# Two of three projection steps moved behind the level's second pair of products in a gated delta rule head

## The chip, the cores and the metric

The kernel runs on one core of one Trainium2 chip (trn2). The metric is the device time of one execution in microseconds, the median of three runs. Differences within 0.2% are about what repeated runs of one kernel show.

## The reference, cut to what matters

The whole program is two transformer blocks in fp32: a gated delta rule block with memory attention and a feed-forward part, then a convolution block and a sparse attention block. The change touches only the gated delta rule (8 heads of 128, 512 tokens). For each head the reference projects the input, runs a short convolution and SiLU over the rows, and solves a unit lower triangular system before it scans over the tokens:

```python
qkv = jax.nn.silu(causal_dwconv(qkv, conv_w))
q, k, v = jnp.split(qkv, [GDN_KW, 2 * GDN_KW], axis=-1)
...
lower = jnp.where(strict, bc[..., :, None] * kk * decay, 0.0)
sol = lax.linalg.triangular_solve(lower + jnp.eye(CHUNK), rhs, left_side=True, lower=True, unit_diagonal=True)
...
v_new = u_n - w_n @ state
o_n = qg_n @ state + p_n @ v_new
state = state * gl_n + kg_n.T @ v_new
```

## The kernel before, in words

The program is written engine by engine, with semaphores between the engines and every engine's order written out by hand. Heads 1 to 6 run as a hardware loop; head 0 and head 7 are peeled (`gdn_tensor`, `gdn_scalar`, `gdn_vector`).

**What one head does.** The triangular matrix is inverted by doubling, in four blocks of 128 tokens side by side in one 128x512 tile. `LEVELS` is 7, so `head_tensor` runs six levels (`lv` 0 to 5). One level is:

1. TensorE forms A from the level's mask of the lower matrix and U, four 128x128 products into bank 4 (line 722).
2. ScalarE copies bank 4 to the tile `As` (line 852).
3. TensorE forms T and As for U into bank 5 (line 730, called U's products here) and, in levels 0 to 4, As and T for T into bank 6 (line 735, T's products).
4. VectorE subtracts bank 5 from `U` (line 931) and bank 6 from `T` (line 934), forms the next mask (line 937), and in between does work for other heads. A of the next level waits for the subtraction of U.

**The projection steps.** While head `h` is inverted, TensorE also computes the projections of head `h+1`: four output tiles (key, value, query, gate z), each of eight steps. One step is three 128x512 products, high by high, high by low and low by high part of the split fp32 numbers (lines 281 to 283). `gap(n)` runs the next `n` of the 32 steps, so the calls of `gap` say where they lie between the head's own products. Nine steps lie ahead of level 0. The second tile ends with step 16, which is the first step of level 2, and the third tile ends with step 24, which is the last step of level 4. Head 7 projects the memory queries in their place.

**What hangs on a finished tile.** ScalarE takes it out of its bank (`take_row`, line 770). VectorE then convolves it over four taps (`conv_steps`): line 799 is the first tap, line 801 the other three, each after a wait for the one before. All of it reads and writes SBUF alone. ScalarE applies SiLU (line 782). GpSimd (POOL) waits for the end of the tile and then splits the weights of the tile after next, a cast (line 226) and a subtraction (line 246), both in SBUF. For the third tile the calls on VectorE stand in the loop over levels:

```python
dve.wait_ge(s_["U_done"], h * 6 + (lv + 1))
V.tensor_tensor(U, U, bank[5], ALU.subtract)   # 931, U_moved
...                                            # 934, 937
conv(lv // 2, 2)                               # two taps of tile lv // 2
```

So the first two taps of the third tile come after T's subtraction in level 4, ahead of U's subtraction in level 5. The last two taps come behind it, then one 128x512 product of the next head's gate rows (line 877), and then the first block of the scan.

**The scan.** Four blocks of 128 tokens follow one another. TensorE forms the new values (line 749, which in block 0 waits for the last subtraction of U), does one step, and waits for VectorE's copy `v_new` (line 952) before line 759 adds to the state. In the scan lie steps 28 to 32.

Of the kernel before, what the change touches and what calls it, by code (L numbers as in the profile page):

```python
# [44 lines left out]
LEVELS = 7  # L45
# [84 lines left out]
def program(nc, t, out):  # L130

    with ExitStack() as ctx:
# [515 lines left out]
        def group_chunks(pe, g):  # L648

            for j in range(GROUP_TILES):  # L650
                unit = g * GROUP_TILES + (seg_g.unit0 + j)
                pe.wait_ge(tile_taken, g * GROUP_TILES + (seg_g.tile0 + j - 1))
                for k in range(DT):
                    products(pe, seg_g, unit, (seg_g.unit0 + j) % 2, 0, bank[(seg_g.tile0 + j) % 2][:, :],
                             lambda k: X_R[:, k], lambda k: X_L[:, k], True, True, ks=(k, k + 1))
                    yield

        def key_norm_tensor(pe, g):
            pe.wait_ge(s_["keys_squared"], g * 2 + 1)
            nc.tensor.matmul(bank[5][:, :], ones, g_["sq_k"][:, :], start=True, stop=True).then_inc(s_["norm_summed"], 1)  # L660

        def query_norm_tensor(pe, g):
            pe.wait_ge(s_["keys_squared"], g * 2 + 2)
            nc.tensor.matmul(bank[6][:, :], ones, g_["sq_q"][:, :], start=True, stop=True).then_inc(s_["norm_summed"], 1)

        def output_norm_tensor(pe, n):

            pe.wait_ge(s_["o_squared"], n)
            nc.tensor.matmul(bank[2][:, :], ones, o_squares, start=True, stop=True).then_inc(s_["o_summed"], 1)

        def head_tensor(pe, h, g, first, last):
            chunks = group_chunks(pe, g)

            def gap(n):
                for _ in range(n):
                    next(chunks, None)

            pe.wait_ge(s_["gate_rows_ready"], h + 1)
            nc.tensor.matmul(bank[4][:, :], ones, g_["D_E"][:, :], start=True, stop=True).then_inc(s_["rows_done"], 1)
            pe.wait_ge(s_["norms_rooted"], h * 2 + 2)  # L680
            pe.wait_ge(s_["silu_done"], h * 3 + 2)
            for b in range(NB):
                mm = nc.tensor.transpose(bank[5][:, b * P:(b + 1) * P], acts[1][:, b * P:(b + 1) * P], ident)
            mm.then_inc(s_["v_turned"], 1)
            gap(1)
            pe.wait_ge(s_["keys_ready"], h + 1)
            for b in range(NB):
                kb = g_["keys"][:, b * P:(b + 1) * P]
                mm = nc.tensor.matmul(bank[7][:, b * P:(b + 1) * P], kb, kb, start=True, stop=True)
            mm.then_inc(s_["kk_done"], 1)  # L690
            for b in range(NB):
                mm = nc.tensor.transpose(bank[6][:, b * P:(b + 1) * P], g_["keys"][:, b * P:(b + 1) * P], ident)
            mm.then_inc(s_["k_turned"], 1)
            gap(4)
            if not first:
                output_norm_tensor(pe, h)
            gap(2)
            pe.wait_ge(s_["T_ready"], h + 1)
            for b in range(NB):
                mm = nc.tensor.transpose(bank[3][:, b * P:(b + 1) * P], g_["T"][:, b * P:(b + 1) * P], ident)  # L700
            mm.then_inc(s_["T_turned"], 1)
            gap(2)
            pe.wait_ge(s_["row_decay_ready"], h + 1)
            pe.wait_ge(s_["v_beta_ready"], h + 1)
            pe.wait_ge(s_["k_gained_ready"], h + 1)
            pe.wait_ge(s_["queries_ready"], h + 1)
            if not first:
                pe.wait_ge(s_["o_rooted"], h)
            for b in range(NB):
                here = slice(b * P, (b + 1) * P)  # L710
                mm = nc.tensor.matmul(bank[2][:, here], g_["keys"][:, here], g_["queries"][:, here], start=True, stop=True)
            mm.then_inc(s_["qk_done"], 1)
            for lv in range(LEVELS - 1):
                joins = g_["low_a"] if lv % 2 == 0 else g_["low_b"]
                pe.wait_ge(s_["low_ready"], h * 6 + (lv + 1))
                if lv == 0:
                    pe.wait_ge(s_["U_ready"], h + 1)
                else:
                    pe.wait_ge(s_["U_moved"], h * 6 + lv)
                for b in range(NB):  # L720
                    here = slice(b * P, (b + 1) * P)
                    mm = nc.tensor.matmul(bank[4][:, here], joins[:, here], g_["U"][:, here], start=True, stop=True)  # L722
                mm.then_inc(s_["A_done"], 1)
                gap(3 if lv < LEVELS - 2 else 1)
                pe.wait_ge(s_["A_ready"], h * 6 + (lv + 1))
                if lv:
                    pe.wait_ge(s_["T_moved"], h * 5 + lv)
                for b in range(NB):
                    here = slice(b * P, (b + 1) * P)
                    mm = nc.tensor.matmul(bank[5][:, here], g_["T"][:, here], g_["As"][:, here], start=True, stop=True)  # L730
                mm.then_inc(s_["U_done"], 1)
                if lv < LEVELS - 2:
                    for b in range(NB):
                        here = slice(b * P, (b + 1) * P)
                        mm = nc.tensor.matmul(bank[6][:, here], g_["As"][:, here], g_["T"][:, here], start=True, stop=True)  # L735
                    mm.then_inc(s_["T_done"], 1)
            gap(2)
            pe.wait_ge(s_["pT_ready"], h + 1)
            pe.wait_ge(s_["q_decayed_ready"], h + 1)
            pe.wait_ge(s_["U_moved"], h * 6 + 6)  # L740
            for b in range(NB):
                here = slice(b * P, (b + 1) * P)
                if b:
                    pe.wait_ge(s_["S_ready"], h * 3 + b)
                    nc.tensor.matmul(bank[7][:, 0:P], g_["keys"][:, here], g_["S"][:, :], start=True, stop=True).then_inc(s_["kS_done"], 1)
                    gap(1)
                    pe.wait_ge(s_["X_ready"], h * 3 + b)
                rhs = g_["X"][:, :] if b else g_["v_beta"][:, here]
                nc.tensor.matmul(bank[2][:, 0:P], g_["U"][:, here], rhs, start=True, stop=True).then_inc(s_["v_done"], 1)
                if b:  # L750
                    nc.tensor.matmul(bank[3][:, here], g_["S"][:, :], g_["q_decayed"][:, here], start=True, stop=False)
                if not last and b == 1:
                    key_norm_tensor(pe, g)
                elif not last and b == 2:
                    query_norm_tensor(pe, g)
                gap(1)
                pe.wait_ge(s_["v_ready"], h * 4 + (b + 1))
                if b < NB - 1:
                    nc.tensor.matmul(bank[4][:, 0:P], g_["k_gained"][:, here], g_["v_new"][:, :], start=True, stop=True).then_inc(s_["S_sum_done"], 1)
                mm = nc.tensor.matmul(bank[3][:, here], g_["v_new"][:, :], g_["pT"][:, here], start=b == 0, stop=True)  # L760
                if b == NB - 1:
                    mm.then_inc(s_["o_done"], 1)
            gap(40)
# [198 lines left out]
        def gdn_tensor(pe):  # L962
            for _ in group_chunks(pe, 0):
                pass
            gates_tensor(pe)
            key_norm_tensor(pe, 0)
            query_norm_tensor(pe, 0)
            head_tensor(pe, 0, 1, True, False)
            with pe.Fori(1, HEADS - 1) as h:
                head_tensor(pe, h, h + 1, False, False)  # L970
            head_tensor(pe, HEADS - 1, HEADS, False, True)
            output_norm_tensor(pe, HEADS)
# [1233 lines left out]
```

## Time and profile before

| what | value |
|---|---|
| median of 3 runs | 2411.93 us (2408.79 to 2413.52) |
| the profiled execution: time, span | 2413.52 us, 2411.6 us |
| PE busy | 2254.8 us, 93% of the span |
| VectorE, ScalarE, POOL busy | 50%, 40%, 32% |
| mean granted clock of TensorE | 0.972 of full speed |
| stretch of the eight heads, from the trace | 124 to 558 us of the span, some 54 us a head |

The engines are named PE (TensorE matmul), PEld (its weight load), DVE (VectorE), ACT (ScalarE), POOL (GpSimd). In a row of the windows each engine's busy time is followed by its count of instructions, in the order PE, PEld, DVE, ACT, POOL, then the granted clock, the share of the DMA engines and GB/s. A row of the timeline has the start in the span, the duration, the engine, the line, the operation, the tiles and how often it is merged; in brackets stands the idle time before it and what ended it. The ends of matmuls are modelled, so the distance between two starts is the better measure of how long PE took.

### The profile page before, as it was taken

What the parts mean: (1) busy time and instruction counts of PE and PEld (TensorE: products, weight loads), DVE (VectorE), ACT (ScalarE), POOL (GpSimd) and SP (SyncE); (2) the same over time, 40 slices, a digit from 0 to 9 for tenths busy, and PEclk for the clock granted to TensorE, in tenths of its full rate; (3) what the DMA queues carried; (4) which work ended last, traced back from release to release, by engine and by line L of the source; (5) the groups of instructions that cost most, each with busy time, mean ns of one, the idle gap of its engine ahead of it and who ended that gap; (6) DMA issues with size and microseconds to landing.
All of it is one profiled execution on the core that took longest, in us unless ns stands there. A gap on an engine that the chain in (4) does not pass through costs nothing.

```text
span 2411.6 us, 31521 instructions
## 1 busy us (share of the span) xinstructions
PE 2254.8 (93%) x10534; PEld 1788.9 (74%) x10534; DVE 1195.1 (50%) x1906; ACT 971.1 (40%) x1612; POOL 768.7 (32%) x336
## 2 busy tenths in 40 slices
PE   3899999998899999989979999999999989999997
PEld 2677777776678888858847888888766657888886
DVE  6366666654243332269964333325566665333322
ACT  4434444433342222265544444222455454444322
POOL 2522222221334444400014444444310103444442
PEclk7999999998999999999989999999999999999999
DMA  3211111111222233211102222322100002322322
GB/s 121 101 36 36 43 35 43 35 38 61 94 70 96 96 99 107 89 44 53 52 19 87 100 96 99 118 99 73 62 18 9 17 10 75 100 96 96 104 99 76
DMA packets 43626, 168.83 MB, mean 70 GB/s; under 512 B 4848, under 2 KB 4912, under 8 KB 43056
## 3 DMA queue, kind: packets, MB, share of 16 engines
q1 hardware_dynamic: 43056, 163.82, 20.3%
q10 hardware_dynamic: 512, 4.24, 0.5%
q8 instruction: 35, 0.57, 0.1%
q14 instruction: 23, 0.19, 0.0%
HBM read 165.95 MB, written 2.10 MB: 70 GB/s over the span
## 4 chain that ended last, share of the span: by engine, by line
PE 80%; DVE 8%; issue 5%; ACT 4%; POOL 1%; DMA 0%; DVEq 0%; ACTq 0%; POOLq 0%; SPq 0%
PE bank L281 21%; PE bank L283 21%; PE bank L282 21%; PE bank L1796 2%; PE bank L722 2%; PE bank L730 2%; PE bank L735 1%; POOL WL L246 1%; ACT Pr L1846 1%; PE bank L1760 1%; PE bank L1778 1%; PE bank L1313 1%; PE bank L1315 1%; PE bank L1314 1%; DVE Pr L1917 1%
## 5 line engine op out<-in xcount | busy, mean ns | idle before, releaser
L246 POOL TENSOR_TENSOR WL<-raw,WR 128x1024 fp32r<-128x1024 f32 (+2 forms) x274 | 706.9, 2580 | 1022.8 <-ACT WR L242 1018.1
L281 PE MATMUL bank<-XR,WR 128*128 128x512 f32 x1528 | 627.6, 411 | 30.1 <-DVE XL L426 15.3
L283 PE MATMUL bank<-XR,WL 128*128 128x512 f32 x1528 | 600.0, 393 | 0.0
L282 PE MATMUL bank<-XL,WR 128*128 128x512 f32 x1528 | 599.0, 392 | 0.0
L242 ACT ACTIVATE WR<-raw 128x1024 fp32r<-128x1024 f32 (+2 forms) x230 | 256.2, 1114 | 754.7 <-PE bank L283 747.1
L281 PEld LDWEIGHTS bank<-XR,WR 128*128 128x128 f32 x1528 | 289.9, 190 | 103.8 <-issue 31.9
L281 PE MATMUL bank<-MR,WR 128*128 128x512 f32 (+1 forms) x856 | 337.4, 394 | 16.1 <-DVE ML L1482 7.5
L282 PEld LDWEIGHTS bank<-XL,WR 128*128 128x128 f32 x1528 | 290.2, 190 | 64.4 <-issue 9.9
L283 PEld LDWEIGHTS bank<-XR,WL 128*128 128x128 f32 x1528 | 289.1, 189 | 62.0
L282 PE MATMUL bank<-ML,WR 128*128 128x512 f32 (+1 forms) x856 | 333.4, 390 | 0.0
L283 PE MATMUL bank<-MR,WL 128*128 128x512 f32 (+1 forms) x856 | 333.2, 389 | 0.0
L226 POOL CAST WR<-raw 128x1024 fp32r<-128x1024 f32 (+1 forms) x58 | 61.7, 1064 | 594.4 <-PE bank L283 509.7
L281 PEld LDWEIGHTS bank<-MR,WR 128*128 128x128 f32 x856 | 163.5, 191 | 52.7 <-issue 13.2
L1269 DVE TENSOR_TENSOR f_up<-bank,R 128x512 f32<-128x512 f32 x66 | 45.6, 691 | 302.7 <-PE bank L283 302.7
L283 PEld LDWEIGHTS bank<-MR,WL 128*128 128x128 f32 x856 | 163.9, 191 | 32.7
L282 PEld LDWEIGHTS bank<-ML,WR 128*128 128x128 f32 x856 | 164.1, 192 | 30.9 <-issue 0.2
L402 DVE TENSOR_TENSOR ACC<-ACC,SQ 128x512 f32<-128x512 f32 (+1 forms) x56 | 86.5, 1545 | 144.0 <-ACT SQ L391 142.7
L1274 DVE TENSOR_TENSOR ML<-f_mid,MR 128x512 f32 x66 | 123.1, 1865 | 64.5 <-ACT MR L1252 64.5
L1212 DVE TENSOR_TENSOR hT<-bank,hT 128x512 f32 (+1 forms) x24 | 16.6, 692 | 161.0 <-PE bank L283 161.0
L1846 ACT ACTIVATE Pr<-Pr,stats 128x512 f32<-128x512 f32 (+3 forms) x128 | 70.3, 550 | 58.2 <-DVE stats L1917 58.2
L1267 DVE TENSOR_TENSOR f_gate<-bank,R 128x512 f32<-128x512 f32 x66 | 45.6, 691 | 92.1 <-PE bank L283 72.0
L426 DVE SCALAR_TENSOR_TENSOR XL<-hT,params,XR (+1 forms) x40 | 69.3, 1733 | 33.8 <-ACT XR L422 33.8
(295 smaller groups left out, 2774.6 us busy)
## 6 DMA issues: line engine op xcount, KB each, us to landing
raw<-w SPq DMA_DIRECT2D x224, 512.0 KB, 3.3
raw<-w SPq DMA_DIRECT2D x48, 704.0 KB, 4.0
raw<-w SPq DMA_DIRECT2D x16, 384.0 KB, 3.0
hT<-xT SPq DMA_DIRECT2D x1, 2048.0 KB, 8.0
hT<-xT ACTq DMA_DIRECT2D x1, 2048.0 KB, 7.9
out<-Y SPq DMA_DIRECT2D x8, 256.0 KB, 2.0
memT<-memT ACTq DMA_DIRECT2D x1, 1024.0 KB, 8.0
phi<-phi ACTq DMA_DIRECT2D x1, 1024.0 KB, 6.1
```

What stands on the lines that cost most here:

```text
L226: nc.gpsimd.tensor_copy(WR[:, here], raw[:, here]).then_inc(high_split, 1)
L242: nc.scalar.activation(WR[:, here], raw[:, here], ACT.Identity).then_inc(high_ahead, 1)
L246: nc.gpsimd.tensor_tensor(WL[:, here], raw[:, here], WR[:, here].bitcast(F32), ALU.subtract).then_inc(weight_split, 1)
L281: nc.tensor.matmul(into, wr, xr(k0 + k), start=start, stop=False)
L282: nc.tensor.matmul(into, wr, xl(k0 + k), start=False, stop=False)
L283: mm = nc.tensor.matmul(into, wl, xr(k0 + k), start=False, stop=stop)
L402: nc.vector.tensor_tensor(ACC[:, 0:width], ACC[:, 0:width], SQ[:, parity * SEQ:parity * SEQ + width], ALU.add).then_inc(summed, 1)
L426: nc.vector.scalar_tensor_tensor(dst, src, gain, high.bitcast(F32), ALU.mult, ALU.subtract).then_inc(input_ready, 1)
L722: mm = nc.tensor.matmul(bank[4][:, here], joins[:, here], g_["U"][:, here], start=True, stop=True)
L730: mm = nc.tensor.matmul(bank[5][:, here], g_["T"][:, here], g_["As"][:, here], start=True, stop=True)
L1274: nc.vector.tensor_tensor(cols(ML, n), f_mid[:, :], cols(MR, n).bitcast(F32), ALU.subtract).then_inc(mid_low, 1)
L1846: ins = nc.scalar.activation(here, here, ACT.Exp, bias=stat(idx, 0)[:, b:b + 1], scale=-1.0, accum_out=stat(idx, 1)[:, b:b + 1])
```

## The change

In `head_tensor` each of levels 0 to 4 had three steps between A and U's products. Now one step lies there, and two lie behind T's products, ahead of the next level's A. Level 5 had one step behind A and two behind the loop; the two now stand inside the loop, at the same place. The order within the 32 steps and their number stay as they are, and no other engine's program is changed.

```diff
@@ -721,7 +721,7 @@
                     here = slice(b * P, (b + 1) * P)
                     mm = nc.tensor.matmul(bank[4][:, here], joins[:, here], g_["U"][:, here], start=True, stop=True)
                 mm.then_inc(s_["A_done"], 1)
-                gap(3 if lv < LEVELS - 2 else 1)
+                gap(1)
                 pe.wait_ge(s_["A_ready"], h * 6 + (lv + 1))
                 if lv:
                     pe.wait_ge(s_["T_moved"], h * 5 + lv)
@@ -734,7 +734,7 @@
                         here = slice(b * P, (b + 1) * P)
                         mm = nc.tensor.matmul(bank[6][:, here], g_["As"][:, here], g_["T"][:, here], start=True, stop=True)
                     mm.then_inc(s_["T_done"], 1)
-            gap(2)
+                gap(2)
             pe.wait_ge(s_["pT_ready"], h + 1)
             pe.wait_ge(s_["q_decayed_ready"], h + 1)
             pe.wait_ge(s_["U_moved"], h * 6 + 6)
```

## Rows read from the trace of the kernel before

**Rows 1.** The page: the chain that ended last, shares of the span by engine.

```profile
PE 80%; DVE 8%; issue 5%; ACT 4%; POOL 1%; DMA 0%; DVEq 0%; ACTq 0%; POOLq 0%; SPq 0%
```

**Rows 2.** Timeline of PE, level 1 of one head and the A of level 2.

```profile
297.80 1.13 PE L722 MATMUL bank<-U,low_b 128*128 128x128 f32 x8
298.69 0.47 PE L281 MATMUL bank<-XR,WR 128*128 128x512 f32 x1
...
300.85 1.05 PE L730 MATMUL bank<-As,T 128*128 128x128 f32 x8
301.74 1.06 PE L735 MATMUL bank<-T,As 128*128 128x128 f32 x8
302.80 1.13 PE L722 MATMUL bank<-U,low_a 128*128 128x128 f32 x8
```

**Rows 3.** Timeline of PE, same head: level 4, level 5, start of the scan.

```profile
312.76 1.13 PE L722 MATMUL bank<-U,low_a 128*128 128x128 f32 x8
...
315.57 0.39 PE L283 MATMUL bank<-XR,WL 128*128 128x512 f32 x1
...
317.72 1.13 PE L722 MATMUL bank<-U,low_b 128*128 128x128 f32 x8
...
319.61 1.15 PE L730 MATMUL bank<-As,T 128*128 128x128 f32 x8
320.52 0.47 PE L281 MATMUL bank<-XR,WR 128*128 128x512 f32 x1
...
321.99 0.38 PE L749 MATMUL bank<-v_beta,U 128*128 128x128 f32 x2
...
324.03 0.49 PE L759 MATMUL bank<-v_new,k_gained 128*128 128x128 f32 x2 [0.96 <-DVE v_new L952]
```

**Rows 4.** Timeline of VectorE in the same head.

```profile
304.04 2.35 DVE L801 SCALAR_TENSOR_TENSOR act<-pre,params,act 128x512 f32<-128x512 f32 x2
...
318.39 1.52 DVE L799 TENSOR_SCALAR act<-pre,params 128x512 f32<-128x512 f32 x1
320.05 0.75 DVE L801 SCALAR_TENSOR_TENSOR act<-pre,params,act 128x512 f32<-128x512 f32 x1
320.93 0.69 DVE L931 TENSOR_TENSOR U<-U,bank 128x512 f32<-128x512 f32 x1
...
323.69 0.28 DVE L952 COPY v_new<-bank 128x128 f32<-128x128 f32 x1
```

**Rows 5.** Timeline of ScalarE in the same head, levels 4 and 5.

```profile
316.00 0.60 ACT L770 ACTIVATE pre<-bank 128x512 f32<-128x512 f32 x1 [1.47 <-PE bank L283]
316.49 0.62 ACT L782 ACTIVATE act<-act 128x512 f32<-128x512 f32 x1
318.89 0.60 ACT L852 ACTIVATE As<-bank 128x512 f32<-128x512 f32 x1 [1.77 <-PE bank L722]
```

**Rows 6.** Timeline of POOL: two splits of this head, one in each of the next two.

```profile
304.81 1.04 POOL L226 CAST WR<-raw 128x1024 fp32r<-128x1024 f32 x1 [9.64 <-PE bank L283]
305.92 2.69 POOL L246 TENSOR_TENSOR WL<-raw,WR 128x1024 fp32r<-128x1024 f32 x1
...
316.13 1.04 POOL L226 CAST WR<-raw 128x1024 fp32r<-128x1024 f32 x1 [7.51 <-PE bank L283]
317.25 2.38 POOL L246 TENSOR_TENSOR WL<-raw,WR 128x1024 fp32r<-128x1024 f32 x1
...
360.30 1.04 POOL L226 CAST WR<-raw 128x1024 fp32r<-128x1024 f32 x1 [9.64 <-PE bank L283]
...
414.11 1.04 POOL L226 CAST WR<-raw 128x1024 fp32r<-128x1024 f32 x1 [9.65 <-PE bank L283]
```

**Rows 7.** Windows at that head's end, and at a later one's: busy by engine, PEclk.

```profile
332.70:336.10 3.40, 2.29 (x11) 1.41 (x10) 1.76 (x4) 3.09 (x5) 3.29 (x2) 1.00 0.00 0
336.10:339.50 3.40, 3.40 (x11) 2.35 (x10) 2.53 (x5) 1.29 (x4) 0.00 (x0) 0.50 0.45 154
445.30:448.70 3.40, 3.40 (x10) 2.18 (x9) 2.43 (x4) 1.19 (x3) 0.04 (x1) 0.51 0.47 154
```

## The prediction

> **What bounds the kernel now.** I read the page first: the chain that ended last is 80% PE and 8% VectorE [rows 1], so what PE does costs its full time, and a change of its order can only win where PE waits. Then I read PE's timeline through one head, level by level, because the diff moves steps there. In level 1, A starts at 297.80, the three steps at 298.69, U's products at 300.85, T's at 301.74, and the next A at 302.80 [rows 2]. The four parts take 0.89, 2.16, 0.89 and 1.06 us, together 5.00. T's products alone would need what U's need, 0.89, so PE stands 0.17 us ahead of the next A, and the wait that the code has there is the one for U's subtraction. A level is otherwise all work: the change has 0.17 us a level to win, five times a head.
>
> Then the tail of the head. Behind the levels PE waits 0.96 us for the copy `v_new` [rows 3], and the VectorE rows say why that is late: the first tap took 1.52 us where the next, with more to read, took 0.75; it ended 0.28 us after POOL's subtraction (317.25 + 2.38 = 319.63), so I take it that it waited for it, then one tap, U's subtraction, two more taps, a 0.7 us product, and the copy, end to end from 318.39 to 323.97 [rows 4, 6]. From 318.4 on, VectorE and not PE sets the time of this head. Six of the other heads (0 to 6 without this one) show the same pattern; head 7 has no taps.
>
> I call A's start of level 4, 312.76, zero of the tail. There the last of the three steps' products starts at 2.81, A of level 5 at 4.96, U's products at 6.85, line 749 at 9.23 and line 759 at 11.27 [rows 3].
>
> **Term 1, the levels.** Removed: 0.17 us ahead of each next A. With two steps there, A comes at the earliest 1.47 us after T's products, and U's subtraction ends long before.
> Added: a wait for `As` ahead of U's products. Level 5 already has one step there and shows the price: A at 317.72, copy 318.89 to 319.49, U's products at 319.61, that is A + 1.89 [rows 3, 5]. A group of two steps takes 321.99 - 320.52 = 1.47, one of three 2.16, so a step takes 0.69 and a group 0.08 on top; one step would let U's products start at 0.89 + 0.77 = 1.66. PE waits 0.23 us. Three steps (2.16) hid the copy wholly. Splitting them into 0.77 + 1.47 = 2.24 costs another 0.08.
> The new level: 1.89 + 0.91 + 0.89 + 1.47 = 5.16 us, where 0.91 is U's products in level 5 (319.61 to 320.52). Before, levels 1 to 4 took (317.72 - 297.80)/4 = 4.98. So +0.18 us a level: the win of 0.17 is paid back by 0.23 + 0.08 and the 0.02 of U's products, with 0.02 for the other levels' shorter wait. For levels 0 to 3 of eight heads that is 32 x 0.18 = 5.8, and head 7's level 4 adds 0.2: **+6 us**. Here two waits are exchanged, and the step count on PE is the same.
>
> **Term 2, what the moved third tile does to the tail (levels 4 and 5 of heads 0 to 6).** The third tile ends with the last step of level 4, which is moved behind U's and T's products. Its last product starts at 5.16 - 0.23 = 4.93 (0.23 is the distance of such products) instead of 2.81, so everything that hangs on the tile is 2.12 us later. In order:
> - ScalarE's take follows by 316.00 - 315.57 = 0.43: 5.36 to 5.96. Its SiLU is issued 0.49 later, and `As` of level 5 can follow at about 6.37. It wants to start at 5.16 + 1.17 = 6.33, so these two ahead of it in ScalarE's queue cost nearly nothing [rows 5]. U's products start at about 7.1.
> - POOL's cast follows by 316.13 - 315.57 = 0.56: 5.49 to 6.53; its subtraction wants to start at 6.60 [rows 6].
> - VectorE's first tap, queued behind T's subtraction, now waits for the take and starts near 6.1, while the cast runs. Level 2 of before shows this meeting: the second tap of the pair from 304.04 should have ended at about 305.7, but ended at 306.39, 0.54 after the cast (305.85), and the subtraction on POOL, issued at 305.92, took 2.69 instead of 2.38, ending 2.22 after the tap [rows 4, 6]. So the two do not share: each waits for the other's whole instruction. The first tap ends at 6.53 + 0.29 = 6.82, and POOL's subtraction about 2.22 later, 9.04. (In before the first tap was the only one that met POOL in the tail.)
> - The second tap, which needs the first one's result, asks at 6.95 and finds POOL inside. It ends 0.55 after it: 9.59. Before, it ended at 320.80, or 8.04 [rows 4].
> - Queued behind it on VectorE: U's subtraction of level 5, the last two taps, the product of line 877, `v_new`. From the end of this tap to line 759 before were 324.03 - 320.80 = 3.23 us. So line 759 starts at 12.82 instead of 11.27: **+1.55 us a head**, seven heads, **+11 us**. PE waits there in two places: for U ahead of line 749 (free at 9.53, U ready at about 10.55) and for `v_new` (about 11.5 to 12.8), 2.3 us together instead of 0.96.
> The subtractions read PSUM and show 0.69 beside POOL too, so I charge them nothing. In the GPSIMD Engine Reference of the Trainium skill, section "Key points", VectorE contends with GpSimd in its two-port modes or with two SBUF inputs; by that rule U's subtraction, with one PSUM input, is indeed free while the taps are not.
> The bounds of this term: nothing, if the tap meets no POOL instruction (VectorE would then reach `v_new` at about the old 11.3), and 2.1 us a head, if the first tap misses the slot between cast and subtraction: it then ends 0.29 after POOL at 8.98, and line 759 is at 8.98 + 0.29 + 0.14 + 0.75 + 3.23 = 13.4. I take 1.55, because level 2's rows show the slot given to VectorE when it asks during the cast.
> The level 2 tile (step 16) is the first of its group before and after, so its take and split keep their place; its taps move off POOL, and POOL falls instead on the mask of line 937, which nobody waits for until level 4.
>
> **Term 3, PE's clock.** In this head the clock fell from full (2.4 GHz) to half (1.2 GHz) at 336.1, just behind a stretch in which PE was busy 2.29 of 3.40 us [rows 7], its gaps 1.11 us together. The head-to-head distance was then 360.30 - 304.81 = 55.49 us, against 414.11 - 360.30 = 53.81 without it [rows 6]: 1.68 us for one half-clock stretch. One more head's end has such a stretch, at 445.3 [rows 7]; I found none at the other heads' ends. After the change, term 2's waits of 1.0 and 1.3 us lie close together with one step between, which is more idle time in one place than ahead of 336.1. I expect one stretch at half clock at nearly every scan's start in heads 0 to 6. Part of it falls on the wait itself and costs nothing, so I take 1.3 us each, from bounds of 0 and 1.68: **+9 us**.
> In TensorE: Matmul & The Clock Gate of the Trainium skill, the section on HAM oscillation asks only that long gaps be avoided, longer than any here; by that rule this term would be zero and the time about 2429. The row at 336.1 already differs from it, since the clock fell there behind gaps of 1.11 us in all. The next section of that page, on a second failure mode, has the clock swing from frequent short idle times too, and by that one the term stands.
>
> The sum: 5.9 + 10.9 + 9.1 = 25.9 us. The profiled execution has a span of 2411.6 and a time of 2413.52; with the sum that is 2439.4. It is the slowest of the three, 1.6 over the median, and the sum on the median is 2437.8. I say **2438 us**.
>
> **The rivals.**
> - *No more half-clock stretches.* For it: most heads of before kept full clock through the same scan. Against: the new gaps are twice as long. Terms 1 and 2 alone: 2411.9 + 16.8 = 2429 us.
> - *The tail hides it.* Only term 1 stays. The tap and POOL would have to miss each other, which 6.1 against 5.49 to 6.53 speaks against. 2411.9 + 5.9 = 2418 us.
> - *The first tap loses the slot.* Term 2 becomes 7 x 2.1 = 15, and the clock term stays: 2442 us. The first tap must start after 6.6, half a microsecond later than I have it; the semaphore and two register steps ahead of it could take part of that.
> - *Within 0.2%.* The copy of `As` is less late than in level 5, and the tail is hidden: the levels then cost 0 to 0.1 us each, 2412 to 2416.
> - *Faster.* One step hides the copy of `As` after all. The place is the wait ahead of U's products; it is decided where a step of 0.77 us outlasts the 1.0 us from A's end to U's start (319.61 - 318.61). If it did, a level would win 0.17 and pay 0.08: 40 x -0.09 = -3.6 us; with the two half-clock stretches of before gone as well (-3.4), 2411.9 - 7.0 = 2405. Level 5's row speaks against it.
>
> **How the numbers follow.** My forecast 0.45; no extra half clock 0.22; only the levels 0.14; the slot lost 0.08; within 0.2% 0.06; faster 0.05. About 0.2%, 4.8 us, is what this kernel's runs can tell from no change, so "only the levels" at 2418 lies just outside it, and I move 0.02 of it inside: faster 0.05, same 0.08, slower 0.87. The range reaches from the levels alone, 2417, to the slot lost with the full 1.68 us for each half-clock stretch, 2412 + 6 + 15 + 12 = 2445, and one or two more stretches at the heads' ends: 2417 to 2447.
>
> **What the changed profile would show.** Term 1: A to A 5.16 us in levels 0 to 3; an idle time of 0.2 us ahead of line 730 put down to `As`; none ahead of line 722. Term 2: line 799 starting during POOL's cast of the third tile and the line 801 behind it stretched to 2.6 us; idle time ahead of line 749 put down to U's subtraction in seven heads; 12.8 us from level 4's A to line 759. Term 3: half clock beginning within some 5 us behind that wait, seven times. I am wrong if level 4's A to line 759 stays near 11.3, if the taps are not stretched, or if U's products start less than 1.8 us behind A.

## The result, and the profile after

The changed kernel takes 2428.42 us (2422.97 to 2431.35), the kernel before 2411.93. The ratio is 1.0069, 95% interval 1.0052 to 1.0087: slower by 16.5 us. The profiled execution has a span of 2424.5 us and a time of 2426.29, 12.9 us of span over the one of before. So the direction was forecast, and the size lies at the rival "no more half-clock stretches" (2429), not at the 2438 of the forecast. In the table of the experiments one run of the kernel before (4144 us) and two of `taps_late` (6911 and 10599 us) stand far above all others and are left out of the ratios, though not of the medians.

PE's timeline, level 2 of the same head (head 3), to be held against [rows 2]. The columns are the same.

```profile
308.89 1.05 PE L722 MATMUL bank<-U,low_a 128*128 128x128 f32 x8
309.69 0.48 PE L281 MATMUL bank<-XR,WR 128*128 128x512 f32 x1
...
310.70 1.15 PE L730 MATMUL bank<-As,T 128*128 128x128 f32 x8
311.69 1.06 PE L735 MATMUL bank<-T,As 128*128 128x128 f32 x8
312.51 0.48 PE L281 MATMUL bank<-XR,WR 128*128 128x512 f32 x1
...
313.98 1.05 PE L722 MATMUL bank<-U,low_b 128*128 128x128 f32 x8
```

A to A is 5.09 us. One step lies between 309.69 and 310.46, and U's products start 1.81 behind A, 0.24 later than the step allows. The two steps behind T's products end where the next A starts, so nothing is waited for there.

VectorE and POOL in the same level:

```profile
308.90 1.64 DVE L801 SCALAR_TENSOR_TENSOR act<-pre,params,act 128x512 f32<-128x512 f32 x2
311.89 0.69 DVE L931 TENSOR_TENSOR U<-U,bank 128x512 f32<-128x512 f32 x1 [1.36 <-PE bank L730]
...
313.39 1.48 DVE L937 TENSOR_TENSOR low_a<-lower,table 128x512 f32<-128x512 f32 x1
```

POOL's subtraction lies from 311.93 to 314.32 there. U's subtraction takes its 0.69 us beside it, and the mask of line 937 ends 0.55 us behind it.

The tail, same head, PE, to be held against [rows 3].

```profile
319.07 1.05 PE L722 MATMUL bank<-U,low_a 128*128 128x128 f32 x8
...
324.17 1.05 PE L722 MATMUL bank<-U,low_b 128*128 128x128 f32 x8
...
326.10 1.15 PE L730 MATMUL bank<-As,T 128*128 128x128 f32 x8 [0.18 <-ACT As L852]
...
329.55 0.46 PE L749 MATMUL bank<-v_beta,U 128*128 128x128 f32 x2 [0.90 <-DVE U L931]
...
331.82 0.69 PE L759 MATMUL bank<-v_new,k_gained 128*128 128x128 f32 x2 [1.11 <-DVE v_new L952]
```

VectorE, the same stretch, to be held against [rows 4].

```profile
325.11 0.71 DVE L799 TENSOR_SCALAR act<-pre,params 128x512 f32<-128x512 f32 x1 [1.45 <-ACT pre L770]
325.96 2.63 DVE L801 SCALAR_TENSOR_TENSOR act<-pre,params,act 128x512 f32<-128x512 f32 x1
328.72 0.69 DVE L931 TENSOR_TENSOR U<-U,bank 128x512 f32<-128x512 f32 x1
...
331.48 0.28 DVE L952 COPY v_new<-bank 128x128 f32<-128x128 f32 x1
```

ScalarE, the take of the third tile, its SiLU and the copy of level 5, against [rows 5].

```profile
324.37 0.60 ACT L770 ACTIVATE pre<-bank 128x512 f32<-128x512 f32 x1 [3.60 <-PE bank L283]
324.86 0.62 ACT L782 ACTIVATE act<-act 128x512 f32<-128x512 f32 x1
325.38 0.59 ACT L852 ACTIVATE As<-bank 128x512 f32<-128x512 f32 x1
```

POOL: the split in level 2 of heads 1 to 3, and the one behind head 3's third tile, against [rows 6].

```profile
197.96 1.04 POOL L226 CAST WR<-raw 128x1024 fp32r<-128x1024 f32 x1 [9.80 <-PE bank L283]
...
254.97 1.04 POOL L226 CAST WR<-raw 128x1024 fp32r<-128x1024 f32 x1 [9.80 <-PE bank L283]
...
310.81 1.04 POOL L226 CAST WR<-raw 128x1024 fp32r<-128x1024 f32 x1 [9.80 <-PE bank L283]
...
324.50 1.04 POOL L226 CAST WR<-raw 128x1024 fp32r<-128x1024 f32 x1 [10.18 <-PE bank L283]
325.62 2.43 POOL L246 TENSOR_TENSOR WL<-raw,WR 128x1024 fp32r<-128x1024 f32 x1
```

Read the four groups from PE's tail to POOL together. The take starts at 324.37, the first tap follows it at 325.11 in the midst of POOL's cast (324.50 to 325.54) and ends 0.28 us behind the cast. The second tap then stands from 325.96 to 328.59, 0.54 us behind the end of POOL's subtraction at 328.05. U's subtraction, which PE waits for, is queued behind that tap. From A of level 4 to line 759 it is 331.82 - 319.07 = 12.75 us, against 11.27 [rows 3]. The waits ahead of line 749 sum to 6.4 us over 7 heads, those ahead of line 759 to 7.7 us over 7 (6.6 before); the first did not exist before.

Windows of PE's clock at this head's scan start, against [rows 7].

```profile
329.00:332.40 3.40, 1.74 (x8) 1.29 (x9) 2.62 (x5) 1.35 (x3) 0.00 (x0) 0.94 0.43 154
332.40:335.80 3.40, 3.40 (x13) 2.77 (x13) 0.94 (x3) 1.19 (x1) 0.00 (x0) 0.56 0.00 0
```

PE had 1.74 us of work in the first window. Its mean granted clock of 0.94 puts the fall to half (1.2 GHz) into its last 0.4 us, at about 332. Such a fall at the scan's start happened in heads 1, 3 and 5 (at about 219, 332 and 445). The casts give the price: head 1 to head 2 is 254.97 - 197.96 = 57.01 us, head 2 to head 3 55.84, so 1.17 us a stretch. The two stretches of before at heads' ends (1.6 to 1.7 each) are gone.

From head 0's first A to head 7's it is 392.8 us (524.15 - 131.40), against 379.3 before (511.37 - 132.07): 13.4 us more. What follows head 7's first A takes 1900.3 us in both traces. In the repeat of the changed kernel the two times are 392.7 and 1903.7 us. So the traces put 13 to 14 us down to the change, and the rest of the 16.5 is not found in the part of the program that was changed.

### The profile page after: what moved, and what is told of

It is laid out like the page before. It is cut to its first block, busy times and chain, and to the rows that moved or that the text cites. A ratio compares the mean times of both kernels' runs of the same rounds, so it can differ in the third digit from the quotient of the medians.

```text
span 2424.5 us, 31521 instructions
## 1 busy us (share of the span) xinstructions
PE 2257.6 (93%) x10534; PEld 1782.7 (74%) x10534; DVE 1204.0 (50%) x1906; ACT 970.3 (40%) x1612; POOL 767.1 (32%) x336
## 4 chain that ended last, share of the span: by engine, by line
PE 79%; DVE 9%; issue 5%; ACT 4%; POOL 1%; DMA 1%; DVEq 0%; ACTq 0%; POOLq 0%; SPq 0%
PE bank L281 21%; PE bank L283 21%; PE bank L282 21%; PE bank L1796 2%; PE bank L730 2%; PE bank L722 2%; PE bank L735 1%; DVE act L801 1%; POOL WL L246 1%; ACT Pr L1846 1%; PE bank L1760 1%; PE bank L1778 1%; PE bank L1313 1%; PE bank L1315 1%; PE bank L1314 1%
```

## The experiments

Each ratio is to the kernel before, run on the same chip (its median there 2411.2 to 2411.6). "A to A" (the mean) and "tail" (A of level 4 to line 759) are of heads 1 to 6 of the trace. "Heads" is the time from head 0's first A to head 7's in the trace, with the count of half-clock stretches inside it. What follows head 7's first A differs by up to 8 us between the traces (1897.6 to 1905.9 us), so this column tells the kernels apart better than the medians do.

| kernel | median us | ratio, 95% interval | A to A, levels 1 to 3 | tail | heads (half-clock stretches) |
|---|---|---|---|---|---|
| before | 2411.93 | | 4.98 | 11.27 | 379.3 (2) |
| changed | 2428.42 | 1.0069, 1.0052 to 1.0087 | 5.09 | 12.75 | 392.8 (3) |
| changed, again | 2427.04 | 1.0066, 1.0048 to 1.0084 | 5.09 | 12.75 | 392.7 (3) |
| levels_0_3 | 2413.42 | 1.0003, 0.9991 to 1.0014 | 5.09 | 11.20 | 379.9 (1) |
| level_4 | 2424.96 | 1.0048, 1.0032 to 1.0064 | 4.97 | 12.83 | 390.1 (2) |
| after_short | 2413.43 | 1.0008, 0.9995 to 1.0020 | 5.09 | 11.31 | 379.3 (0) |
| before_short | 2412.66 | 0.9997, 0.9982 to 1.0011 | 4.98 | 11.16 | 378.8 (2) |
| after_filler | 2424.05 | 1.0053, 1.0034 to 1.0072 | 5.09 | 12.75 | 389.2 (0) |
| after_taps_late | 2413.65 | 1.0019, 1.0006 to 1.0032 | 5.09 | 11.47 | 379.7 (0) |
| two_one | 2408.41 | 0.9987, 0.9971 to 1.0003 | 4.76 | 11.20 | 369.9 (0) |
| taps_late | 2403.01 | 0.9964, 0.9948 to 0.9979 | 4.98 | 10.14 | 369.2 (1) |
| taps_late_2_1 | 2392.00 | 0.9929, 0.9909 to 0.9948 | 4.76 | 10.09 | 361.4 (0) |

**Which levels cost: levels_0_3.** Against the kernel before:

```diff
-                gap(3 if lv < LEVELS - 2 else 1)
+                gap((1, 1, 1, 1, 3, 1)[lv])
...
-            gap(2)
+                gap((2, 2, 2, 2, 0, 2)[lv])
```

> One step ahead of U's products and two behind in levels 0 to 3 alone; level 4 keeps its three steps ahead. Theory (two terms: a wait for As in each level, and a third tile that ends late): only the first term is left, 5.09 against 4.97 us from A to A in levels 1 to 4, so about +4 us, 2416; from A of level 4 to line 759 stays 11.27 us; the tap of line 801 after the first is not stretched; no half clock at a scan's start. Rival (the split of the levels alone costs, wherever it stands): four fifths of the change's 16.5 us, +13 us, with the tail of the head longer too.

PE's timeline, head 3:

```profile
315.98 1.05 PE L722 MATMUL bank<-U,low_a 128*128 128x128 f32 x8
...
327.18 0.49 PE L759 MATMUL bank<-v_new,k_gained 128*128 128x128 f32 x2 [0.94 <-DVE v_new L952]
```

The tail stays short (11.20 us) and the first tap is again the only one in it that meets POOL. The split levels are longer, 5.09 us, and level 4 with its three steps is 0.08 shorter than before (4.88), so a head without half clock takes 54.25 us against 53.9. Over seven heads that is some 2.4 us. It does not show in the time of this trace's heads (379.9 us against 379.3) because one half-clock stretch at a head's end, at 283.1, stands there in place of two. The median moved by less than can be told. The rival is out: the split of the levels costs a little, and it is not where most of the 16.5 us lie.

**Level 4 alone: level_4.** The same two lines with `(3, 3, 3, 3, 1, 1)` and `(0, 0, 0, 0, 2, 2)`.

> The split in level 4 alone. Theory: the tail is whole, 12.75 instead of 11.27 us from A of level 4 to line 759 in seven heads, +10.5 us, and some heads have half clock at the scan's start (0 to 4, 1.2 us each) in place of the two at heads' ends before: +8 to +14 us, 2420 to 2426. Rival (the levels cost, the tail little): +3 us.

```profile
319.86 1.13 PE L722 MATMUL bank<-U,low_a 128*128 128x128 f32 x8
...
332.69 0.49 PE L759 MATMUL bank<-v_new,k_gained 128*128 128x128 f32 x2 [1.12 <-DVE v_new L952]
```

One level out of five brings 13.4 of the 16.5 us in the medians and 10.8 of the 13.4 in the traces' heads, and the tail is 12.83 us. The trace has no half clock at a scan's start, although the waits are the same as in the changed kernel (0.90 us ahead of line 749 and 1.12 ahead of line 759). It has two stretches at heads' ends, as before; this is the window of the first:

```profile
232.50:235.90 3.40, 3.40 (x12) 2.38 (x11) 2.41 (x5) 1.15 (x4) 0.00 (x0) 0.53 0.51 154
```

**Is it POOL, or the late take: after_short.** The changed kernel with POOL's subtraction cut short in this stage. It leaves out 7/8 of the low parts of the projection weights, which stay stale.

```diff
-            low_unit(seg, slot)
+            low_unit(seg, slot, P if seg is SEG["gdn"] else None)
...
-        def low_unit(seg, slot):
-            here = slice(slot * SLOT, slot * SLOT + seg.kt * P)
+        def low_unit(seg, slot, cut=None):
+            here = slice(slot * SLOT, slot * SLOT + (cut or seg.kt * P))
```

> The changed kernel, with POOL's subtraction (line 246) for the weights of the gated delta rule's projections done on 128 of 1024 columns, so that the rest of the low parts is stale; the cast stays whole. Theory (the taps wait for POOL's whole instruction): the second tap takes 0.75 instead of 2.63 us, PE's waits ahead of lines 749 and 759 shrink, 11.2 to 11.4 us from A of level 4 to line 759 instead of 12.75, and the time is 10 us under the changed kernel's, about 2417. Rival (it is the late take of the tile and not POOL): 12.5 us or more stays, and the time is within 3 us of the changed kernel's 2428.

PE, VectorE and POOL of head 3, one timeline each:

```profile
314.20 1.05 PE L722 MATMUL bank<-U,low_a 128*128 128x128 f32 x8
...
325.50 0.49 PE L759 MATMUL bank<-v_new,k_gained 128*128 128x128 f32 x2 [0.85 <-DVE v_new L952]
```

```profile
320.21 0.71 DVE L799 TENSOR_SCALAR act<-pre,params 128x512 f32<-128x512 f32 x1 [1.43 <-ACT pre L770]
321.07 0.75 DVE L801 SCALAR_TENSOR_TENSOR act<-pre,params,act 128x512 f32<-128x512 f32 x1
322.39 0.69 DVE L931 TENSOR_TENSOR U<-U,bank 128x512 f32<-128x512 f32 x1 [0.57 <-PE bank L730]
```

```profile
320.73 0.51 POOL L246 TENSOR_TENSOR WL<-raw,WR 128x128 fp32r<-128x128 f32 x1
```

The first tap still meets the cast (0.71 us), the second runs free in 0.75, U's subtraction now waits for PE rather than PE for it, and the tail is 11.31 us. The take is as late as in the changed kernel, so lateness alone does not make the tail long: it is the whole length of POOL's subtraction that the tap waits through. The time came down by 15 us, more than the 10 expected. Seven tails of 1.44 are 10.1 us, and the three half-clock stretches are gone too, which is 3.5 more. That brings the heads to the 379.3 us of the kernel before, but not for the same reason: this kernel still pays the longer levels, and it has no half clock where the kernel before has two stretches.

**The same cut on the kernel before: before_short.**

> The kernel before with the same short subtraction on POOL. Theory: the first tap of the third tile takes 0.48 instead of 1.52 us, but U's subtraction then waits for PE's products, so only 0.2 us a head comes back, -1.6 us or within the noise: 2410. Rival (the contention sets the tail of the kernel before as well): 1.04 us a head, -7 us, 2405.

```profile
316.82 0.48 DVE L799 TENSOR_SCALAR act<-pre,params 128x512 f32<-128x512 f32 x1
...
319.24 0.69 DVE L931 TENSOR_TENSOR U<-U,bank 128x512 f32<-128x512 f32 x1 [1.04 <-PE bank L730]
```

The first tap is 1.04 us shorter and U's subtraction waits 1.04 us for PE instead: the tail gives back only 0.11. In the kernel before, POOL's contention filled a wait that was there anyway.

**Where the tail's time lies: taps_late and after_taps_late.** The last two taps and the gate row product move on VectorE into its idle times in the scan. taps_late has it on the kernel before, after_taps_late on the changed one:

```diff
-                conv(lv // 2, 2)
-            if not last:
-                gate_rows_vector(g)
+                if lv < 5:
+                    conv(lv // 2, 2)
...
                 V.tensor_copy(g_["v_new"][:, :], bank[2][:, 0:P]).then_inc(s_["v_ready"], 1)
+                if b == 1:
+                    conv(2, 2)
+                if b == 2 and not last:
+                    gate_rows_vector(g)
```

> The kernel before, with two taps of the third tile moved on VectorE from level 5 to behind the v_new of the scan's second block, and the product of line 877 to behind that of the third. Theory (VectorE's queue ahead of v_new sets the tail in both kernels): 10.2 instead of 11.27 us from A of level 4 to line 759 in seven heads, the wait ahead of line 759 gone, -7 us, 2404.5. Rival (the scan has no room for them: the SiLU and the query squares come late for line 664, or the state's subtraction waits for a tap): the gain is lost again within the scan, within 3 us of 2411.6.

> The changed kernel with the same late taps. Theory: the second tap still waits for POOL's subtraction and holds back U's subtraction of level 5 (wait of 0.9 us ahead of line 749 stays), but v_new no longer stands behind two taps and a product: 11.5 us from A of level 4 to line 759 instead of 12.75, -8.5 us, about 2420. Rival (line 759 is late for another reason than VectorE's queue): 12.5 us or more stays.

after_taps_late, PE and VectorE of head 3 (line 951 is `v_new`'s copy here):

```profile
315.36 1.05 PE L722 MATMUL bank<-U,low_a 128*128 128x128 f32 x8
...
325.84 0.46 PE L749 MATMUL bank<-v_beta,U 128*128 128x128 f32 x2 [0.93 <-DVE U L931]
...
326.83 0.38 PE L759 MATMUL bank<-v_new,k_gained 128*128 128x128 f32 x2
```

```profile
322.25 2.63 DVE L801 SCALAR_TENSOR_TENSOR act<-pre,params,act 128x512 f32<-128x512 f32 x1
```

Both came out as the theory has it: tails of 10.14 and 11.47 us, and the scan had room. taps_late saves 0.36%. In after_taps_late the stretched tap and the wait ahead of line 749 stay, and the wait for `v_new` is gone. So the tail has two parts: the tap that waits for POOL and holds back U's subtraction, and the queue ahead of `v_new`. Without the change only the second part limits. after_taps_late came out lower than expected (2413.65 for 2420): beside the 9.0 us of the tails (7 x 1.28) its trace also lacks the three half-clock stretches, 3.5 us.

**Two steps ahead, one behind: two_one.** `(2, 2, 2, 2, 3, 1)` and `(1, 1, 1, 1, 0, 2)` in the kernel before.

> Levels 0 to 3 with two steps ahead of U's products and one behind T's, level 4 with three ahead as in the kernel before. Theory: two steps (1.47 us) outlast the copy of As (1.0 us after A's end), and the one behind covers U's subtraction, so neither wait is left; the split costs 0.08 us: 4.89 us from A to A against 4.97, tail as before: 32 x -0.08 = -2.5 us, 2409, hardly outside the noise. Rival (the split itself costs more than the wait ahead of A): 5.0 us or more from A to A.

PE, level 0 of head 3:

```profile
290.20 1.06 PE L722 MATMUL bank<-U,low_a 128*128 128x128 f32 x8
291.01 0.47 PE L281 MATMUL bank<-XR,WR 128*128 128x512 f32 x1
...
292.48 1.05 PE L730 MATMUL bank<-As,T 128*128 128x128 f32 x8
293.37 1.06 PE L735 MATMUL bank<-T,As 128*128 128x128 f32 x8
294.18 0.48 PE L281 MATMUL bank<-XR,WR 128*128 128x512 f32 x1
...
294.96 1.05 PE L722 MATMUL bank<-U,low_b 128*128 128x128 f32 x8
```

A level takes 4.76 us, 0.13 less than expected, with no wait in it. The reason is in the rows: an fp32 group that did not wait, followed by a step, takes 0.81 us to the next start and not 0.89 (A at 290.20, the step at 291.01; T's products 293.37 to 294.18). The head distance falls by some 0.9 us, from 53.9 to 53.0. The measured 0.13% is not clear of the noise by itself (its runs spread over 15 us), so the gain is shown by the trace alone.

**Both: taps_late_2_1.**

> Both of the others in one kernel: two steps ahead and one behind in levels 0 to 3, and the late taps. Theory: the two gains add, -10 us, 2402. Rival: within 2 us of the late taps alone.

```profile
304.44 1.05 PE L722 MATMUL bank<-U,low_a 128*128 128x128 f32 x8
...
313.62 0.38 PE L749 MATMUL bank<-v_beta,U 128*128 128x128 f32 x2
314.53 0.38 PE L759 MATMUL bank<-v_new,k_gained 128*128 128x128 f32 x2
```

2392.0 us, 0.71% under the kernel before and the fastest of all. A head takes 51.8 us (53.9 before), 2.1 us less. The medians of the two parts add up to only 12 of the 19.6 us, but in the traces the parts do add: without the half-clock stretches (1.6 to 1.7 us each) the heads take 376.0 us before, 369.9 in two_one, 367.6 in taps_late and 361.4 here, that is 6.1 and 8.4 less for the parts and 14.6 for both. The rest of the 19.6 lies in half-clock stretches and outside the heads; which share the change has in that, no run shows.

**What halves the clock: after_filler and after_again.** The changed kernel with one product more where PE waits for U; its result is not used.

```diff
+            pe.wait_ge(s_["T_moved"], h * 5 + 5)
+            nc.tensor.matmul(bank[6][:, :], ones, g_["queries"][:, :], start=True, stop=True)
             pe.wait_ge(s_["pT_ready"], h + 1)
```

> The changed kernel with one more product on PE, ones by queries, 128x512 in fp32 into bank 6 (free there), ahead of the wait for U's last subtraction: 0.9 us of work in the place of the 0.9 us of waiting ahead of line 749. Its result is overwritten later. Theory (the half clock at the scan's start follows from PE's two waits close together): no half clock at any scan's start, 12.8 us from A of level 4 to line 759 as in the changed kernel, every head 55.8 us instead of three with 57.0, so 0 to 4 us under the changed kernel's time. Rival (the half clock comes from something else, at set places): still about three heads of 57 us, and the time equal or up to 7 us more.

> The changed kernel once more, unaltered, beside the one with the added product. Theory: between 0 and 4 half-clock stretches at scans' starts by chance of the phase, 12.75 us from A of level 4 to line 759 in heads 1 to 6 as before; 2428, within 3 us. Rival (the places of the half clock are set by the program): the same three heads, 1, 3 and 5.

after_filler, PE of head 3 (lines of the scan are two higher here):

```profile
328.37 1.02 PE L739 MATMUL bank<-queries,table 128*128 128x512 f32 x2
329.46 0.46 PE L751 MATMUL bank<-v_beta,U 128*128 128x128 f32 x2
...
331.73 0.49 PE L761 MATMUL bank<-v_new,k_gained 128*128 128x128 f32 x2 [1.12 <-DVE v_new L954]
```

after_again, windows:

```profile
276.70:280.10 3.40, 3.40 (x13) 2.79 (x13) 0.93 (x3) 1.22 (x1) 0.00 (x0) 0.55 0.00 0
389.30:392.70 3.40, 3.40 (x14) 2.86 (x14) 0.70 (x3) 1.46 (x2) 0.00 (x0) 0.54 0.00 0
```

With the wait ahead of line 749 filled, none of heads 0 to 6 has a half-clock stretch, all of heads 1 to 5 take 55.8 us, and the mean granted clock from 124 to 570 us is 1.00 against 0.98. The heads take 3.6 us less than in the changed kernel, three stretches of 1.17; head 7, which has no such wait, pays 0.86 us for the added product. The medians differ by 3.0 us, which the intervals of the two ratios do not separate. Unaltered, the changed kernel has three stretches again, in heads 2, 4 and 6 this time, so which heads they hit is not set by the program. That the idle time makes them is well supported: the three traces with both waits in full have six stretches at 21 scan starts, the other nine none at 63. after_filler alone does not show it, because level_4, with both waits, has none either. What decides whether a head is hit stays open.

## Why the prediction was right, and where its size was off

**What bounds the kernel** held: the time came from PE's waits. The chain that ended last has 9% VectorE after and 8% before [rows 1], and line 801 has 1% of it.

**Term 1, the levels: right kind, 6.0 us forecast, 3.2 measured.** U's products start 1.81 behind A (1.89 forecast) and A to A is 5.09 (5.16). A and T's products each take 0.08 less than forecast: I took 0.89 from groups that had waited or were followed by another such group, and an fp32 group ahead of a step takes 0.81. U's products, which wait for `As` and have another fp32 group behind them, take 0.99 where I had 0.91, and that eats one of the two. That also means that the wait ahead of each A in the kernel before was worth more than the 0.17 I read, about 0.25 (1.06 - 0.81), as two_one shows. I also took all heads alike. Levels 0 to 3 together grew by about 0.47 us in heads 1 to 6, by 0.06 in head 0 and by 0.22 in head 7, whose level 4 added 0.05: 3.2 us in all.

**Term 2, the tail: right, 10.9 us forecast, 10.3 measured.** Each step came at its place: the take 5.30 behind level 4's A (5.36 forecast), the first tap during the cast at 6.04 (6.1), the second stretched to 2.63 (2.64), U's subtraction behind it, line 759 at 12.75 (12.82). That the tap's wait for POOL's subtraction is the cause, and not the late tile alone, is shown by after_short; that it is the move of level 4's steps is shown by level_4. The choice of the slot between the cast and the subtraction, against the rival that the tap loses it, held in all seven heads. In the GPSIMD Engine Reference of the Trainium skill, section "Key points", contention is said of VectorE instructions with two SBUF inputs or in two-port modes. The trace agrees for the tap of line 801, which reads two tiles in SBUF and waits (2.63 us), and for U's subtraction, which reads one and shows 0.69 beside POOL in level 2 (311.89). The first tap reads one tile and waits as well (0.71 us); by that section it would have to be in a two-port mode, which no run here shows.

**Term 3, the clock: stretches came, but fewer, and the term is near nothing.** The step that failed: "I expect one stretch at half clock at nearly every scan's start in heads 0 to 6 ... I take 1.3 us each". The profile of after has three, after_again three, at 1.17 us each, and level_4, with the same waits, none. And I left out that the stretches of before can go: the two at heads' ends (3.3 us) did not occur in either trace of the changed kernel. Why they did not stays open. Net, the term is near 0 (3 x 1.17 - 3.3 = +0.2) and not +9.1. This error of 9 us is nearly the whole distance from 2438 to 2428.4. The rival that priced it at zero came out, though for another reason than it gave: the clock does fall, but as much is lost before as after. That the two nearly cancel is chance as far as the runs show, so the rival's 2429 is in part luck.

The sum with measured terms is 3.2 + 10.3 + 0.2 = 13.7 us, between the 12.9 of the two spans and the 16.5 of the medians.

**The level 2 tile** went as written: its two taps from 308.90 took 1.64 us where they took 2.35 [rows 4], and the mask of line 937 took up the meeting with POOL (1.48 us) and held nothing back.

**The faster case** did not occur: the copy of `As` takes 1.0 us from A's end, and one step of 0.77 does not cover it. Two do (two_one), and then the split is a gain in the trace.

## What to carry to other kernels

Splitting cover between two waits pays only if each part still outlasts its wait: against two steps and one (4.76 us a level, no wait), three at one wait lost 0.22 us and one and two lost 0.33. Before moving work on the bounding engine, list who takes its results and what those engines have queued next: here the moved steps cost 0.12 us a level, while the tile that ended 2 us later cost 1.5 us a head by putting a VectorE instruction against a long POOL one, with the critical subtraction behind it. An instruction that need not stand ahead of a critical copy should stand behind it, in the idle time of the chain that follows: that was worth 1.1 us a head, with PE's order untouched.

## What the runs showed of the hardware that was not expected

VectorE and POOL hand SBUF access over by whole instructions with fixed tails: in every head of both kernels a waiting tap of line 801 ended 0.54 to 0.55 us behind POOL's instruction, one of line 799 0.28 or 0.29 us behind it. A tap that asked during the cast was let in ahead of POOL's subtraction, in seven heads of seven.

Inside the heads PE's clock fell to half behind stretches with idle times of no more than 1.12 us each, and not every time: identical waits gave 3, 3 and 0 stretches in seven heads. Each stretch is worth 1.2 to 1.7 us, so kernels that differ by some 4 us in 2400 are told apart better by the head distances of the trace than by their medians.
